# Moving the identity products of x into the last contraction of each expert layer

## The reference

```python
x = layer_norm(ALPHA * x + (1.0 + g_m) * y, mix_ln_g[i], mix_ln_b[i])
h = x * (1.0 + sc_f) + sh_f
y = hierarchical_moe(h, r_w_group[i], r_b_group[i], r_w_expert[i], r_b_expert[i],
                     e_w_gate[i], e_w_up[i], e_w_down[i])
x = layer_norm(ALPHA * x + (1.0 + g_f) * y, ffn_ln_g[i], ffn_ln_b[i])
```

## Time and profile before

| | |
|---|---|
| executions | 1999.14, 1998.64, 1993.16 us |
| median | 1998.64 us |
| span of the profiled execution | 1995.7 us |
| its TensorE busy | 1879.8 us (94%) |
| its VectorE busy | 854.2 us (43%) |
| its ScalarE busy | 329.8 us (17%) |
| read from HBM | 597.67 MB |

### The profile page before, as it was taken

One profiled execution on the slowest core, in us unless ns is written; L12 is line 12 of the kernel. 1 busy time (PEld: TensorE's weight loads), 2 busy tenths in 40 slices (PEclk: granted clock), 3 DMA queues, 4 the chain that ended last, 5 costly groups with the idle time before them and its releaser, 6 DMA issues.

```text
span 1995.7 us, 21050 instructions
## 1 busy us (share of the span) xinstructions
PE 1879.8 (94%) x8098; PEld 957.2 (48%) x8098; DVE 854.2 (43%) x1546; ACT 329.8 (17%) x782; POOL 87.6 (4%) x129
## 2 busy tenths in 40 slices
PE   8998999999999999999999999989999988989887
PEld 4555665455556654856334334333875323323322
DVE  1476898834768887854111111112325111111102
ACT  2452111133521102122001000001002000000000
POOL 4102000001020001100000000000000000000000
PEclk9999999999999999999999999999999999999999
DMA  9315887661168877566999999999345999999996
GB/s 305 102 59 171 301 288 269 241 190 43 59 215 291 296 294 233 176 234 239 393 422 431 433 429 431 432 428 407 143 198 229 423 432 432 431 431 432 431 428 266
DMA packets 134376, 603.11 MB, mean 302 GB/s; under 512 B 15288, under 2 KB 59240, under 8 KB 119936
## 3 DMA queue, kind: packets, MB, share of 16 engines
q1 hardware_dynamic: 128512, 591.41, 74.6%
q0 software_dynamic: 4880, 10.22, 1.9%
q10 hardware_dynamic: 880, 0.07, 0.0%
HBM read 597.67 MB, written 1.10 MB: 300 GB/s over the span
## 4 chain that ended last, share of the span: by engine, by line
PE 62%; DMA 26%; DVE 5%; issue 1%; DVEq 1%; ACT 1%; ACTq 1%; POOL 1%; SPq 0%
PE ps L2582 15%; DMA ring<-in_e_w_up 13%; PE ps L944 13%; DMA ring<-in_e_w_gate 11%; PE ps L646 5%; PE ps L1027 5%; PE ps L2396 4%; PE ps L2600 3%; PE ps L2326 3%; PE ps L2411 2%; PE ps L745 2%; PE ps L2515 2%; PE ps L2500 1%; ACTq L1144 1%; DMA ring<-in_e_w_down 1%
## 5 line engine op out<-in xcount | busy, mean ns | idle before, releaser
L2582 PE MATMUL ps<-ring,hT 128*64 128x512 f32 (+1 forms) x1056 | 240.4, 608 | 33.9 <-DMA ring<-in_e_w_gate 17.5
L2600 PE MATMUL ps<-ring,qkT 128*64 128x512 f32 (+1 forms) x1024 | 226.6, 594 | 8.4 <-ACT qkT L2818 7.5
L2582 PE MATMUL ps<-ring,late 128*32 128x512 f32 (+1 forms) x928 | 212.3, 611 | 20.0 <-DMA ring<-in_e_w_up 12.1
L2582 PEld LDWEIGHTS ps<-ring,hT 128*64 128x64 f32 (+1 forms) x1056 | 77.7, 126 | 193.0 <-issue 192.9
L646 PE MATMUL ps<-ring,hT 128*128 128x512 f32 (+1 forms) x384 | 169.0, 584 | 0.0
L3115 DVE TENSOR_TENSOR qkT<-ps,qkT 128x512 f32<-128x512 f32 (+1 forms) x64 | 44.2, 690 | 254.0 <-PE ps L2600 254.0
L3138 DVE TENSOR_TENSOR qkT<-ps,qkT 128x512 f32<-128x512 f32 (+1 forms) x32 | 22.1, 690 | 290.7 <-PE ps L2582 290.7
L2582 PEld LDWEIGHTS ps<-ring,late 128*32 128x32 f32 (+1 forms) x928 | 66.4, 126 | 159.3 <-issue 158.9
L2600 PEld LDWEIGHTS ps<-ring,qkT 128*64 128x64 f32 (+1 forms) x1024 | 69.7, 123 | 145.7 <-issue 145.7
L1652 DVE SCALAR_TENSOR_TENSOR qkT<-ring,cc,qkT 128x512 f32<-128x512 f32 x168 | 125.8, 749 | 8.6 <-issue 0.4
L3134 DVE TENSOR_TENSOR x<-ps,x 128x1024 f32<-128x1024 f32 x22 | 26.9, 1225 | 196.3 <-PE ps L2500 196.3
(11 more groups left out here) (444 smaller groups left out, 2211.6 us busy)
## 6 DMA issues: line engine op xcount, KB each, us to landing
ring<-in_e_w_up SPq DMA_DIRECT2D x28, 4096.0 KB, 21.8
ring<-in_e_w_down SPq DMA_DIRECT2D x28, 4096.0 KB, 19.4
ring<-in_e_w_gate SPq DMA_DIRECT2D x26, 4096.0 KB, 21.6
ring<-in_ada_w SPq DMA_DIRECT2D x24, 2048.0 KB, 14.1
ring<-in_w_gate SPq DMA_DIRECT2D x16, 1408.0 KB, 8.1
ring<-in_w_up SPq DMA_DIRECT2D x16, 1408.0 KB, 9.0
ring<-in_w_down SPq DMA_DIRECT2D x22, 1024.0 KB, 5.0
ring<-in_e_w_gate SPq DMA_DIRECT2D x8, 2048.0 KB, 14.2
```

Of the source, the lines that this page charges most:

```text
L2582: last = mm(dst, xg[:, j, at + x * n_tok:at + x * n_tok + place], w(x, j), start=(j == 0), stop=(j == KC - 1))
L2600: lasts[x] = mm(dst, m.hidT[:, j, rows + x * place:rows + (x + 1) * place], half_of(w(x, j), n), start=(j == 0), stop=(j == 3))
```

## The change

The four identity products move. In the case of one round, they are issued inside `contract` of the last pair, after the half that needs slot 2 and before the wait for slot 3 (`held()`, called from there). In the case of more rounds they are issued after the loop. What remains behind the branch are the four `last_combine` calls. Banks 4 and 5 are still in use during the contraction, so tile 1's sum moves from banks 4 and 5 to banks 2 and 3, those of gate and up; tile 0's stays in 6 and 7. `tile_bank` for the transposes ahead of layer 1 is laid out anew to fit, and so are the reads on VectorE and the bank of the two unread products. VectorE's, ScalarE's and SyncE's instructions keep their number and order.

```diff
 def tile_bank(at, i, b):
 
-    return b + 4 * i if at in (AT_FINAL, AT_EXP0) else b
+    if at == AT_EXP0:
+        return (0, 1, 4, 5)[b] + 2 * i
+    return b + 4 * i if at == AT_FINAL else b
+
+
+def tail_bank(i, n):
+
+    return (6, 2)[i] + n
...
+        def held():
+
+            pe.wait_ge(t["acc"], 2 * n_combines)
+            pe.wait_ge(t["gwt"], n_combines + 1)
+            for i in range(TILES):
+                for n in range(2):
+                    mm(m.ps[:, tail_bank(i, n), :], m.ident[:], half_of(m.x[:, i, :], n), start=True, stop=False)
+
...
                 if by_halves(p):
                     terms(0, (0, 1))
                     used(p, DOWN, terms(1, (0, 1))[1])
+                    if last_round and p == N_PAIRS - 1:
+                        held()
                     arrived(p, DOWN, 1)
                     terms(0, (2, 3))[1].then_inc(t["down_half"], 1)
                     used(p, DOWN + 1, terms(1, (2, 3))[1])
...
+            pe.wait_ge(t["gwt"], rounds * n_combines + 1)
+            pe.sem_inc(m.seen, 1)
+            pe.wait_ge(t["acc"], rounds * n_combines * 2)
+            pe.sem_inc(m.seen, 1)
+            held()
         with pe.Else():
-            one_round(0, True, LAST_PAIRS)
+            one_round(0, True, LAST_PAIRS, True)
         done = rounds * N_PAIRS
-        done_c = rounds * n_combines
-        pe.wait_ge(t["gwt"], done_c + 1)
-        pe.sem_inc(m.seen, 1)
-        pe.wait_ge(t["acc"], done_c * 2)
-        pe.sem_inc(m.seen, 1)
-
-        def held(i, n):
-            mm(m.ps[:, 6 - 2 * i + n, :], m.ident[:], half_of(m.x[:, i, :], n), start=True, stop=False)
 
         def last_combine(i, n):
-            mm(m.ps[:, 6 - 2 * i + n, :], m.GwT[:, i, :], half_of(m.ye, n), start=False, stop=True).then_inc(t["tail_ps"], 1)
-
-        held(0, 0)
-        held(0, 1)
+            mm(m.ps[:, tail_bank(i, n), :], m.GwT[:, i, :], half_of(m.ye, n), start=False, stop=True).then_inc(t["tail_ps"], 1)
+
         for n in range(2):
             pe.wait_ge(t["ye"], done * 2 + (n + 1))
             pe.sem_inc(m.seen, 1)
             last_combine(0, n)
         for n in range(2):
-            held(1, n)
             last_combine(1, n)
```

More of the change, by code:

```diff
@@ L2501, in combine, with one_round @@
             last.then_inc(t["comb"], 1)
-        def one_round(r, first, pairs):
+        def held():
[4 more added lines that the diff above has]
+                    mm(m.ps[:, tail_bank(i, n), :], m.ident[:], half_of(m.x[:, i, :], n), start=True, stop=False)
+        def one_round(r, first, pairs, last_round=False):
             def gather(q, k):
@@ L2587, in expand, with contract @@
                 used(p, first + 1, last)
-            def contract(p):
+            def contract(p, last_round):
                 w = weights(p, DOWN, 4)
@@ L2660, in one_round @@
                 pe.sem_inc(m.seen, 1)
-                contract(p)
+                contract(p, last_round)
         one_round(0, True, range(0, 2))
@@ L2692, in second_tensor @@
         for n in range(2):
-            held(1, n)
             last_combine(1, n)
         if l == 0:
-            unread(2, 3)
+            unread(2, 1)
         if l == 0:
@@ L3162, in gained @@
             def gained(i, n):
-                stt(half_of(m.x[:, i, :], n), m.ps[:, 6 - 2 * i + n, :], st[:, 28 + 2 * i:29 + 2 * i], half_of(m.exp_g, n), ALU.subtract, ALU.mult)
+                stt(half_of(m.x[:, i, :], n), m.ps[:, tail_bank(i, n), :], st[:, 28 + 2 * i:29 + 2 * i], half_of(m.exp_g, n), ALU.subtract, ALU.mult)
             def shifted_out(i, n):
@@ L3192, in tail @@
             dve.wait_ge(t["tail_ps"], 4 * l + 2 * i + n + 1)
-            v.bn_stats(st[:, (2 * i + n) * 6:(2 * i + n + 1) * 6], m.ps[:, 6 - 2 * i + n, :])
+            v.bn_stats(st[:, (2 * i + n) * 6:(2 * i + n + 1) * 6], m.ps[:, tail_bank(i, n), :])
         if l == 1:
@@ L3205, in second_vector @@
         variance(1)
-        normalise(4 * l + 4, 1, banks(m, 4, 2))
+        normalise(4 * l + 4, 1, banks(m, tail_bank(1, 0), 2))
         for i in range(TILES):
```

## The result

The changed kernel takes 2004.45 us (median of 14 executions, 1997.01 to 2006.49). The kernel before, executed 14 times as well by then, takes 1997.45 us (1991.44 to 2002.11). The medians alone differ by 0.35%; the ratio of the executions is put at 1.0028, with a 95% interval of 1.0019 to 1.0036, which is 3.8 to 7.2 us. The forecast was 2004.7 us, 1.0031. The profiled execution took 2003.48 us and its span is 2001.5 us, where the earlier trace rows has 1995.7.

A forecast was written before the change was run, and what follows sets the result against it. At layer 0's end VectorE's code fetch behind its branch was taken to bound, with no later slack to absorb a delay. 3.7 + 0.8 + 1.6 = +6.1 us on 1998.64 gave 2004.7 us, range 2000.5 to 2008.5.

The forecast's parts named there:

- Rival A: Layer 0: the branch isn't what holds VectorE; layer 0 gains 0.6 us, layer 1 loses 1.4: +0.8 us, 1999.4; chance 0.12.
- C: Both layers: identity products are free, filling a wait for weights; at the very most −6.9 us, 1991.8; chance 0.03.
- D: Slower by layer 1 alone, the mixer's stream hiding layer 0's delay: +1.6 us, 2000.2; chance 0.10.
- Rival B: VectorE's code fetch shows behind the branch in both layers: +7.3 us, 2005.9; chance 0.17.
- The price of the four in the middle: Last contraction: four identity products between its halves, with the return to the narrow ones, take 3.7 us.
- Layer 0 on VectorE: End of layer 0: second `scaled_out`, branch, fetch and first `bn_stats` all move later, and the mixer with them: +3.7 us.
- The clock: Layer 0, before the transposes: TensorE idle about 4.1 us, so its clock falls; +0.8 us, bounds 0 and 1.6.
- Layer 1: End of layer 1: VectorE starts later and ends last; +1.4 us, bounds 1.1 to 2.8, taken as 1.6.
- The sum: Whole kernel: 3.7 + 0.8 + 1.6 = +6.1 us, giving 2004.7 us on the median of 1998.64.

The follow-up runs named there:

- e3: Kernel before, with VectorE's branch and its code for further rounds taken out: ratio 0.9997 (0.9984 to 1.0010), whole stretch −1.6 us.
- e1: Changed kernel with the identity products moved into the last contraction in layer 0 alone: ratio 1.0021 (1.0008 to 1.0034) to the kernel before.
- e4: Changed kernel with VectorE's branch and its code for further rounds taken out: ratio 1.0005 (0.9994 to 1.0016) to the kernel before.
- e2: Changed kernel with the identity products moved into the last contraction in layer 1 alone: ratio 1.0007 (0.9994 to 1.0020) to the kernel before.
- e7: Changed kernel with four unread products in place of two behind layer 0's combines: one execution, whole stretch +3.1 us against the kernel before.
- e10: The kernel of e7 again, timed beside e9: median 2004.05 us, ratio 1.0021 (1.0010 to 1.0033) to the kernel before.
- e9: Changed kernel unchanged, profiled and timed a second time: median 2001.71 us, ratio 1.0019 (1.0008 to 1.0029) to the kernel before.
- e6: On top of e5, tile 0's two identity products moved into TensorE's waits in the last pair: 1996.48 us, ratio 0.9991 to the kernel before.
- e5: Kernel before, with VectorE's branch moved ahead of the last two pairs: ratio 0.9995 (0.9984 to 1.0007), whole stretch −1.0 us.
- e8: Changed kernel with VectorE's branch moved ahead of the last two pairs: ratio 1.0004 (0.9995 to 1.0013) to the kernel before.

## Why the prediction was right

**The cause was.** That VectorE's code fetch and not the combine holds the first `bn_stats` in layer 0 was argued from a gap and a branch record; e3 shows it by taking the branch away. That a delay of `scaled_out` goes through to the end is shown too: the stretch between the layers kept its length (574.4 us in the changed kernel, 574.6 before), and e1 alone is slower. Rival A falls with e3; e4 is the kernel that it describes, and there layer 0 comes out 0.65 us shorter than in the kernel before (19.84 in place of 20.49), where A had worked out 0.6. C falls with the result, and D with e1. Rival B, a fetch in layer 1 as well, falls with e3 and e4, where layer 1 keeps its length without the branch, and with the changed kernel's trace: its branch there is at 1988.7, `bn_stats` starts at 1989.74, and the instruction queue's only packet of that time is at 1989.9, behind that start. The first row is the branch, the second the queue from 1989.7 to 1990.1 us:

```profile
L3166 DVEq COMPARE_BRANCH  x2: 72/72/72, 1391.7 to 1988.7; - x2
q14 instruction: 1, 0.01, 6.5%
```

So `bn_stats` didn't wait for this packet: its instruction was on the core already. The rule of the Trainium skill (Runtime: NRT & Kernel Launch, section Instruction fetch mechanics) puts the stall down to targets outside the pages held; the traces are in keeping with it, with a stall in layer 0, where VectorE jumps over the longer round, and none in layer 1. Where the page boundaries lie, and so whether the targets are outside and inside them, isn't shown.

**The terms, one by one.**

- *The price of the four in the middle*, 3.7 us: 3.8. The second half starts 7.22 us after the first, and the second `scaled_out` 10.92 us after the contraction's start in place of 7.12.
- *Layer 0 on VectorE*, +3.7 us: this is the term that was mis-sized. `scaled_out` and the branch moved by 3.8 us as forecast, but the fetch didn't keep its length. From branch to first instruction it took 5.8 us in the kernel before and 5.9 in e2, but 4.1 to 4.2 in the changed kernel, e7 and e10, and 5.4 to 5.5 in e1 and e9. So the term is 2.1 to 3.5 us.
- *The clock*, +0.8 us: 0 to 0.8. TensorE was idle ahead of the transposes for 2.51 us in the changed kernel, 3.89 in e1 and 3.80 in e9, where about 4.1 were forecast. The fall came in these three and not in e7 and e10, which have four unread products; it lasted well into the mixer in e1, and by a little in e9 (0.97 over the mixer's first 3.4 us).
- *Layer 1*, +1.6 us: 1.25. I had 1.4 from the rows and added to it for the fetch, which isn't there. The wait for `ye` was there; the second `bn_stats` started 0.1 us earlier than worked out, and the chain behind it took 3.01 us for 3.09.
- *The sum*, 6.1 us: 3.2 to 4.7 by the traces, 7.0 by the first medians, 5.6 and 3.8 by the two ratios. That 2004.7 came so close to 2004.45 is in part luck: the forecast stood on a median of three executions, 1998.64, that was 1.2 us above that of fourteen, and the first timing of the changed kernel lies above what its traces and its second timing account for. The right statement of what the change costs is 3 to 6 us.

**What the change did in the end.** It fills 0.25 us of a wait for weights in layer 1 and nothing in layer 0, and pays with 3.8 us in layer 0 (3.3 in layer 1) on the `scaled_out` that stands ahead of all that VectorE has still to do.

## What to carry to other kernels

Work that is moved forward to fill a wait must stand in the wait, as in layer 1 of e6; and layer 0 of e6 shows that even there it can make a load start later and lose the gain again. In front of a half of a contraction that has its weights, it delays the engine that reads the result, and a shorter tail behind doesn't give it back. When an engine starts late after a branch, compare the end of what it is said to wait for with its own start. A difference of some us can be its code being fetched, as the 3 to 5 us here were; a packet of the instruction queue in the gap speaks for it, and the kernel without the branch shows it. In e5 and e8 the branch cost nothing that the trace shows once it stood where VectorE waits anyway. Parts of a few us in a kernel whose executions lie 6 us or more apart are better measured as stretches of the traces, from a common point, than by medians.

## What the runs showed that I had not expected

- The length of the fetch behind the same branch in layer 0 came in two groups, 4.1 to 4.2 and 5.4 to 5.9 us. The packet of the instruction queue is seen 2.1 to 2.2 us behind the branch in the first and 3.4 to 3.8 in the second, and the 2.0 to 2.1 us from the packet to `bn_stats` are the same in both; so only the time until the packet differs. In all of them the DMA engines are full then. In layer 1's end, where no other load runs, the packet is there 1.2 us behind the branch in both the kernel before and the changed one; but no run takes the loads away from layer 0, so that they are the cause isn't shown. The shorter ones are all of kernels with the products moved, but so are two of the longer ones; what decides was not found.
- The start of layer 0's last contraction, with the same work ahead of it, lay anywhere from 1372.67 us (e2) to 1383.09 (e10), 10.4 us apart. It goes with TensorE's clock ahead of that point: over the stretch 0 to 1370 us the granted clock is 1.00 in the first and 0.99 in the second, and of the changed kernel's executions the one with a mean clock of 0.992 took 1997.01 us, the one with 0.985 2006.49.
